# Another order of ScalarE's work on the memory in the first values stage

## The reference

```python
h = _rmsnorm(x, a_norm_attn[i])
z = h @ a_w_in[i]                       # queries, keys, values, memory queries
...
kv = _rmsnorm(mem, mem_norm) @ w_mem_kv # memory keys and values, in every layer
```

## Time and profile before

| | |
|---|---|
| median of 3 runs | 1176.01 us (1175.8 to 1176.9) |
| profiled execution | 1175.98 us, span 1174.2 us |
| busy: TensorE matmul / VectorE / ScalarE / GpSimd | 1154.3 / 893.1 / 757.8 / 340.5 us |
| chain that ended last | TensorE 82%, VectorE 10%, ScalarE 3% |

### The profile page before, as it was taken

The page is one execution under the profiler, slowest core; times in us unless marked ns, Lnnn a source line. Parts: engine busy times, 40 slices in busy tenths (PEclk is TensorE's granted clock), DMA queues, the critical chain, the costliest instruction groups (busy, mean ns, idle before and its releaser), DMA issues.

```text
span 1174.2 us, 26850 instructions
## 1 busy us (share of the span) xinstructions
PE 1154.3 (98%) x9150; PEld 1086.4 (93%) x9150; DVE 893.1 (76%) x1491; ACT 757.8 (65%) x1373; POOL 340.5 (29%) x303
## 2 busy tenths in 40 slices
PE   9999999999999999999999999999999999999998
PEld 8888999999998999999998779999889978999987
DVE  7788777666578877756659979999556776899964
ACT  7766655444565755554557878888556666988852
POOL 3320355300012245522302205555000310455500
PEclk9999999999999999999999999999999999999999
DMA  9554566655655466665654445666745643566673
GB/s 327 176 156 140 178 197 197 197 188 192 215 157 161 147 197 197 198 214 187 203 183 132 139 143 182 197 197 202 228 159 170 241 148 126 187 201 197 202 218 105
DMA packets 64056, 216.64 MB, mean 185 GB/s; under 512 B 7777, under 2 KB 10993, under 8 KB 63985
## 3 DMA queue, kind: packets, MB, share of 16 engines
q1 hardware_dynamic: 63808, 215.17, 56.7%
q10 hardware_dynamic: 176, 0.54, 0.2%
HBM read 211.47 MB, written 1.06 MB: 181 GB/s over the span
## 4 chain that ended last, share of the span: by engine, by line
PE 82%; DVE 10%; ACT 3%; issue 2%; POOL 1%; DMA 1%; SPq 0%; DVEq 0%; POOLq 0%; ACTq 0%
PE bank L785 16%; PE bank L786 16%; PE bank L787 16%; PE bank L712 4%; PE bank L714 4%; PE bank L713 4%; PE bank L661 3%; DVE w_lo L1601 3%; PE bank L663 3%; PE bank L662 3%; PE bank L590 2%; PE bank L591 2%; PE bank L596 1%; PE bank L915 1%; PE bank L932 1%
## 5 line engine op out<-in xcount | busy, mean ns | idle before, releaser
L1601 DVE TENSOR_TENSOR w_lo<-raw,w_hi 128x1024 fp32r<-128x1024 f32 x386 | 505.5, 1318 | 75.1 <-ACT w_hi L1139 73.8
L1139 ACT CAST w_hi<-raw 128x1024 fp32r<-128x1024 f32 x386 | 402.1, 1046 | 239.5 <-PE bank L787 100.9
L785 PE MATMUL bank<-h_hi,w_hi 128*128 128x256 f32 x1184 | 326.9, 276 | 0.4
L786 PE MATMUL bank<-h_lo,w_hi 128*128 128x256 f32 x1184 | 325.6, 275 | 0.0
L787 PE MATMUL bank<-h_hi,w_lo 128*128 128x256 f32 x1184 | 325.6, 275 | 0.0
L785 PEld LDWEIGHTS bank<-h_hi,w_hi 128*128 128x128 f32 x1184 | 227.3, 192 | 1.4 <-DVE h_lo L1675 1.2
L786 PEld LDWEIGHTS bank<-h_lo,w_hi 128*128 128x128 f32 x1184 | 227.3, 192 | 0.1
L787 PEld LDWEIGHTS bank<-h_hi,w_lo 128*128 128x128 f32 x1184 | 227.3, 192 | 0.0
L785 PE MATMUL bank<-a_hi,w_hi 128*128 128x256 f32 x544 | 150.1, 276 | 1.2 <-DVE a_lo L1675 1.1
L786 PE MATMUL bank<-a_lo,w_hi 128*128 128x256 f32 x544 | 149.6, 275 | 0.0
L787 PE MATMUL bank<-a_hi,w_lo 128*128 128x256 f32 x544 | 149.6, 275 | 0.0
(11 more groups left out here) (222 smaller groups left out, 2107.7 us busy)
## 6 DMA issues: line engine op xcount, KB each, us to landing
raw<-in_w_up_sb SPq DMA_DIRECT2D x44, 512.0 KB, 3.4
raw<-in_w_up_fox SPq DMA_DIRECT2D x44, 512.0 KB, 3.5
raw<-in_w_up_a SPq DMA_DIRECT2D x32, 512.0 KB, 3.5
raw<-in_w_down_a SPq DMA_DIRECT2D x32, 512.0 KB, 4.6
raw<-in_w_up_b SPq DMA_DIRECT2D x32, 512.0 KB, 3.4
raw<-in_w_down_b SPq DMA_DIRECT2D x32, 512.0 KB, 4.7
raw<-in_w_in_sb SPq DMA_DIRECT2D x24, 512.0 KB, 3.7
raw<-in_w_in_fox SPq DMA_DIRECT2D x24, 512.0 KB, 3.5
```

Of the source, the lines that this page charges most:

```text
L785: nc.tensor.matmul(dst, w_hi[:, slot, w], in_turns(src_hi[:, at + k, :]), start=begin, stop=False)
L786: nc.tensor.matmul(dst, w_hi[:, slot, w], in_turns(src_lo[:, at + k, :]), start=False, stop=False)
L1139: nc.scalar.copy(w_hi[:, slot, 0:k * P], raw[:, slot, 0:k * P]).then_inc(hi_ready, 1)
L1601: nc.vector.tensor_tensor(w_lo[:, slot, 0:k * P], raw[:, slot, 0:k * P], w_hi[:, slot, 0:k * P].bitcast(f32), ALU.subtract).then_inc(lo_re ...
```

## The change

On ScalarE the squares begin one unit earlier: 0 and 1 at s = 1, 2 and 3 at s = 2, 4 and 5 at s = 3 (ahead of the norm of `x` and of the v_tok copies), 6 and 7 at s = 4. Operand tiles 4 to 7 of `mem_b` move from s = 1 to s = 5, behind the split and ahead of the last v_tok copies. On VectorE the low parts of tiles 4 to 7 move from behind unit s = 1 to behind s = 5, that is to the end of the stage. TensorE's wait for all of `h2_lo` goes. No work is added or left out.

```diff
             values("in_a")
-            pe.wait_ge(h_lo, operand_count("mem_b", 0, 0, KT - 1))
-
             def memory_values():
...
                     split(0, RING, g["unit"] + s + RING, KT)
+                    if name == "in_a" and s == 3:
+                        memory_squares(4)
                     if s == MS_AFTER[name]:
                         norm_scale(columns=True)
                     if name == "in_sb" and s == MS_AFTER[name]:
                         norm_scale()
-                    if name == "in_a" and s < 2:
-                        memory_operand(s)
-                    if name == "in_a" and s in (2, 4, 5):
-                        memory_squares((0, None, 4, 6)[s - 2])
+                    if name == "in_a" and s in (0, 5):
+                        memory_operand(s // 5)
+                    if name == "in_a" and s in (1, 2, 4):
+                        memory_squares((0, 2, None, 6)[s - 1])
...
-                    if name == "in_a" and s == 3:
-                        memory_squares(2)
...
-            values("in_a", {1: lambda: [low("mem_b", ZM, h2_hi, h2_lo, 0, 0, k) for k in range(KT)]})
+            values("in_a", {1: lambda: [low("mem_b", ZM, h2_hi, h2_lo, 0, 0, k) for k in range(KT // 2)],
+                            5: lambda: [low("mem_b", ZM, h2_hi, h2_lo, 0, 0, k) for k in range(KT // 2, KT)]})
```

## The result

The kernel after the change takes 1178.23 us (median of 15 runs, 1177.44 to 1179.42), the kernel before 1176.14 (15 runs beside them): a ratio of 1.0017, interval 1.001 to 1.0024, or +2.09 us. The prediction was 1178.6. The profiled execution after has a span of 1176.5 us, before 1174.2. Lines have moved by one or two: the splits of VectorE are at 1599, the squares at 1149, the additions at 2108, the v_tok copies at 1379, lam_exp at 1546.

The account below looks back on a forecast made before the run. TensorE, busy 98% of the span, was taken as the bound. It loses 2.5 before tile 0 and about 1.4 before tile 2, regains 1.17 and 0.1: 2.6 us on 1175.98, so 1178.6 us, range 1176.8 to 1179.9.

Parts of the forecast that it names:

- Steps 1 and 2: ScalarE's first two memory squares start at 29.52 and 29.84; VectorE's next two splits run gapless from 30.40 for 2.3 us.
- Step 3: GpSimd's first two additions: first gets in, second waits, ending 33.9; or first waits for both splits, second ending 34.2.
- an addition of about 2 us: Sign expected in the profile after: a GpSimd addition lasting about 2 us, between 30 and 34.
- Steps 4 and 5: Held additions delay ScalarE's squares: norm at 36.0 or 36.3, 2.4 to 2.7 later; TensorE waits about 2.5 before tile 0.
- Step 6: TensorE's wait of 1.17 us before the memory's mean square goes; the last addition ends at 42.1 to 42.4.
- Step 7: VectorE's moved low parts end at 43.6 to 43.9, lambda steps take 1.22, lam_exp comes 2.5 to 2.8 us later.
- Step 8: Everything behind lam_exp keeps its order, 2.5 to 2.8 us later; TensorE's 1.0 us wait for scaled memory stays.
- Step 9: Removing TensorE's wait at line 998 is worth nothing by itself; the shifted weight transfers cost nothing.
- No holding: Rival: GpSimd's additions take 0.74 each whatever VectorE does; v_tok 0.15 late, time 1175.8; chance 0.13.
- Strict turns: Rival: a waiting GpSimd addition gets in after every VectorE split; 3.0 to 3.2 us lost, 1179.1; chance 0.15.
- Taken back later: Rival: a later TensorE wait absorbs part of the delay; half taken back gives 1177.3; chance 0.15.
- The clock: Rival: TensorE's gaps of 2.5 and 1.4 bring its lower clock for 14 matmuls, 2.7 us more, 1181.3; chance 0.05.

Follow-up runs that it names:

- e7b: Changed kernel with six f32 matmuls of ones filling TensorE's gap ahead of tile 0; 1178.59 us against 1176.06 for the kernel before.
- e5: Changed kernel with VectorE's lambda steps moved ahead of its last four low parts; 1178.33 us against 1176.41 for the kernel before.
- e7: Changed kernel with twelve matmuls of ones in TensorE's gap ahead of tile 0; 1180.39 us against 1176.41 for the kernel before.
- e57: Changed kernel with lambda steps first and twelve matmuls of ones in TensorE's gap; 1179.88 us against 1176.41 for the kernel before.
- e57b: Changed kernel with lambda steps first and six matmuls of ones in TensorE's gap; 1177.82 us against 1176.06 for the kernel before.
- e3: Changed kernel with GpSimd's eight memory additions replaced by writes of a constant; 1175.0 us against 1176.31 for the kernel before.
- e4: Kernel before with GpSimd's eight memory additions replaced by writes of a constant; 1174.33 us against 1176.31 for the kernel before.
- e1: Kernel before with only TensorE's wait at line 998 removed; 1176.44 us against 1176.31 for the kernel before.
- e6b: Against the kernel before: squares 0 and 1 early, operand tiles 4 to 7 at s = 2, squares 2 and 3 at s = 3; 1175.42 us against 1176.41.
- e6c: Against the kernel before: squares 0 and 1 early, operand tiles 4 to 7, squares 2 and 3 at s = 2, lambda at s = 4; 1175.02 against 1176.06.
- e2: Changed kernel with VectorE's low parts 2 and 3 moved between the splits of units 9 and 10; 1177.53 us against 1176.31 for the kernel before.

## Why the prediction was right

The mechanism and its chain held, and the time lies in the range. The costlier of the two orders came (2.8), and the lambda steps were taken 0.7 too dear: 2.1 where 2.6 was forecast. Two things were luck. The choice of 2.6, nearer an order that never came, made up for 0.2 of the 0.7. And the clock fell, which had a chance of 0.05: that its 1.63 us on TensorE didn't show in the time is nothing that the prediction had worked out.

- Steps 1 and 2, right: S0 and S1 began at 29.64 (forecast 29.52), the two splits ran together from 30.54 (30.40).
- Step 3: of its two orders, the second came in the profile after: A0 passed over by both splits (until 33.47, forecast 33.2 to 33.4 by 32.6 + 0.74), A1 at the end of 34.35 (34.2). The order that I took as the likelier one, A0 in and A1 waiting for both splits, occurred in none of the six profiles with this order of squares and splits. After and e7b had A0 passed over; in e5, e7, e57 and e57b A0 got in, and then the turns were strict, as the rival has it. e7 and e7b have the same order on these three engines and A0 ready at the same moment of it (1.71 and 1.70 after the first of the four h_lo), and went different ways, so which it is isn't set by the program's order. What sets it stays open. By its own numbers the prediction's sign, "an addition of about 2 us", should have read 2.8 (A1 in the first order, 31.09 to 33.9) or 3.3 (A0 in the second, 30.08 to 33.3); 3.29 came. The reading of the earlier trace rows was right for one addition behind one split and said nothing on what two splits in a row do next.
- Steps 4 and 5, right for that order: the norm at 36.39 (36.3), tile 0 at 38.98 (38.9), a wait of 2.65 (about 2.5). e3 shows the cause: take the holding away, and the norm is back.
- Step 6, right in its result: the wait ahead of line 851 is gone. The mean square began at 46.04 and not at the 44.5 of the forecast, for the clock; in e7b, at full speed, it begins 14.70 behind the mean square of `x`, which is 44.63 on the scale of the profile after.
- Step 7 is where the size failed. h_lo ended at 43.95 (43.9), but the lambda steps took 43.87 to 44.61, not 1.22 but 0.74. Before, they stood beside GpSimd's additions, and the pair of products took 0.82:

```profile
39.72 0.82 DVE L2042 TENSOR_TENSOR lam_prod<-lam_in_sb 128x64 f32<-128x64 f32 x2
```
```profile
38.80 4.14 POOL L2109 TENSOR_TENSOR rstd_mem<-rstd_mem,square 128x256 f32<-128x256 f32 x4 [0.16 <-POOL rstd_mem L2109]
```

  At their new place no addition was running, and the pair took 0.34:

```profile
43.94 0.34 DVE L2041 TENSOR_TENSOR lam_prod<-lam_in_sb 128x64 f32<-128x64 f32 x2
...
44.87 0.16 DVE L2046 TENSOR_TENSOR neg_lam<-lam_exp 128x1 f32<-128x1 f32 x1 [0.27 <-ACT lam_exp L1546]
...
45.26 0.42 DVE L1618 TENSOR_TENSOR Z<-bank,rstd 128x256 f32<-128x256 f32 x1
```

  neg_lam took 0.16 where it had 0.46, for the same reason. e4 shows that it was the additions: there the steps stand where they stood before, beside writes in place of additions, and take 0.35 and 0.16. So lam_exp moved by 2.36, and the eviction of tile 0 by 45.26 - 43.18 = 2.08. The forecast moved both by 2.8 in this order. Durations that a neighbour had lengthened were carried to a place without that neighbour: 2.8 - 2.08, 0.7 us too much, is the term that was mis-sized.
- Step 8, right in kind: from lam_exp on the order is the old one, and 2.08 is carried to the end. Line 876 came at 49.77 (about 50.3), its wait at 0.46, not 1.0, since TensorE was itself late by the clock (1.02 in e7b, without the lower clock).
- Step 9, right: e1 measured the removed wait at nothing, and in the profile after ScalarE waits for no transfer up to 75 us.
- The rivals. No holding: refuted by the 3.29 us of A0 and by e3. Strict turns: real, in four of six profiles, from S0 to the norm 6.95 where it had 6.98 worked out (29.52 to 36.5), yet its 1179.1 has the same oversized lambda steps; up to the norm it costs 0.2 more than the second order. Taken back later: no, from line 876 to the end it is 1126.5 before and 1126.7 after. The clock: by their mean clock nine of the 15 runs had it, and it was given 0.05 at a price of 2.7; its price on TensorE was 1.63, and in the time none that shows, as it lay under VectorE's delay. The 2.7 came from the 14 slow matmuls at the start, and there the profile before has a granted clock of 1.00 (0 to 10 us): that they ran at the lower level isn't shown, and what slowed them stays open. The argument against it, that the gap of 1.17 had kept the fast pitch, did not carry to a gap of 2.65.
- The prediction held it likelier (0.62) that the kernel is slower by over 0.2%, which is 2.35 us; +2.09 lies just below. That chance rested on the 2.6, and falls with the term of step 7.

The page "SBUF — State Buffer" of the Trainium skill, section "Who interferes with whom", has the one that began first keep the other out for its whole length; it doesn't say who goes next when both have work waiting. In e5 the records fit that with strict turns. In the profile after A0 waited through a second split that began after it had been waiting, 3.29 us in all. So the prediction's reading of the page as strict turns is more than the page says, and the measurements show both.

## What to carry to other kernels

Before moving GpSimd work, look at which VectorE instructions will run beside it: among short operand steps an addition took 0.74 us, among long splits in a row 1.5 to 3.5, and every engine that waits for its buffers pays. When an instruction is moved, take its duration from a row that has the neighbours of its new place, not of its old one. And before repairing one late engine, ask which other is as late: here, by the profiles, the clock and the lambda steps each hid the other, and removing either alone won nothing.

## What was unexpected of the hardware

- Two outcomes of the same contention: of six profiles, two with the first addition passed over twice (3.29 us in the kernel after), four with strict turns, with A0 ready 0.44 us before the operand steps' end in both (30.18 against 30.62 in the kernel after, 30.91 against 31.35 in e5). e6b and e6c have the same order up to A0, with one split behind it: in e6b A0 got in, in e6c it was passed over (2.16).
- After a gap of 2.65 us TensorE ran at full speed for about 1 us (38.98 to 39.9), then for about 3.4 us at 0.50 (by the PEclk column), and was back at 43.3 without having stood still. After one of 1.57 (e2) and one of 0.84 (e6b) no such stretch shows, and in the profile of e5 none after 3.05, although eight of the 11 runs of e5 have the lower mean clock (none of e2, one of e6b).
- A write of a constant on GpSimd isn't held by splits (e3: two in 0.74 us beside three of them), an addition, which reads, is.
